# MLA stage: the second retention pair's weights and the first output columns loaded from ScalarE's DMA queue instead of SyncE's

## What is computed

```python
h = _rms_norm(x, attn_norm[layer])
(d_q, d_k, d_v, m_cq, m_ckv, m_krope, r_q, r_k, r_v, r_g) = _split_cols(h @ w_in[layer])
o_diff = _diff_attention(...)      # 4 heads
o_mla = _mla(...)                  # 4 heads: softmax attention over low-rank q, k, v
o_ret = _retention(...)            # 4 heads, in chunks of 128 tokens, with a running state
mixed = jnp.concatenate([o_diff, o_mla, o_ret], axis=-1)
x = x + mixed @ w_out[layer]
h = _rms_norm(x, ffn_norm[layer])
x = x + (jax.nn.silu(h @ w_gate[layer]) * (h @ w_up[layer])) @ w_down[layer]
```

## Time and profile before

| | us |
|---|---|
| median of 3 runs | 2638.94 (2637.67 to 2639.61) |
| the profiled execution: its own time | 2640.68 |
| the profiled execution: span of the profile | 2638.8 |
| PE busy | 2540.5 (96%) |
| DVE, ACT, POOL busy | 1543.5, 1091.1, 1005.8 |

### The profile page before, as it was taken

The page is one execution under the profiler, slowest core; times in us unless marked ns, Lnnn a source line. Parts: engine busy times, 40 slices in busy tenths (PEclk is TensorE's granted clock), DMA queues, the critical chain, the costliest instruction groups (busy, mean ns, idle before and its releaser), DMA issues. The chain is left out here.

```text
span 2638.8 us, 43248 instructions
## 1 busy us (share of the span) xinstructions
PE 2540.5 (96%) x13148; PEld 2179.0 (83%) x13148; DVE 1543.5 (58%) x3050; ACT 1091.1 (41%) x2507; POOL 1005.8 (38%) x1149
## 2 busy tenths in 40 slices
PE   6999989999999999999999999999999999999997
PEld 5999977878788888888889998777887888888886
DVE  4667555472655455577757765555637445445786
ACT  4444544362522222344444545444534332223444
POOL 3455422174254544301044554223823544451011
PEclk9999999999999999999999999999999999999998
DMA  5111011023232333473341101012222233327533
GB/s 182 29 34 36 19 38 39 21 72 144 72 108 94 101 114 109 154 288 96 95 130 32 35 20 41 6 39 91 97 80 89 79 115 107 112 83 269 190 96 120
DMA packets 238682, 242.68 MB, mean 92 GB/s; under 512 B 27936, under 2 KB 171040, under 8 KB 238496
## 3 DMA queue, kind: packets, MB, share of 16 engines
q1 hardware_dynamic: 237968, 238.34, 28.1%
q10 hardware_dynamic: 528, 2.10, 0.2%
HBM read 172.75 MB, written 67.63 MB: 91 GB/s over the span
## 5 line engine op out<-in xcount | busy, mean ns | idle before, releaser
L2533 POOL TENSOR_TENSOR fw_a_lo<-fw_a_raw,fw_a_hi 128x512 fp32r<-128x512 f32 x132 | 178.6, 1354 | 455.1 <-DVE fw_s_raw L2105 455.1
L2533 POOL TENSOR_TENSOR fw_s_lo<-fw_s_raw,fw_s_hi 128x512 fp32r<-128x512 f32 x176 | 232.2, 1332 | 55.2 <-ACT fw_s_hi L1583 55.2
L745 PE MATMUL banks<-ht_hi,da_hi 128*128 128x512 f32 x496 | 192.9, 389 | 0.0
L745 PE MATMUL banks<-ht_lo,da_hi 128*128 128x512 f32 x496 | 192.9, 389 | 0.0
L745 PE MATMUL banks<-ht_hi,da_lo 128*128 128x512 f32 x496 | 192.9, 389 | 0.0
L745 PE MATMUL banks<-w_diff_hi,ht_hi 128*128 128x384 f32 x512 | 179.6, 351 | 2.3 <-DVE dv L1816 2.0
L745 PE MATMUL banks<-w_diff_hi,ht_lo 128*128 128x384 f32 x512 | 171.9, 336 | 0.0
L745 PE MATMUL banks<-w_diff_lo,ht_hi 128*128 128x384 f32 x512 | 171.6, 335 | 0.0
L2361 POOL TENSOR_TENSOR qk_rot<-rope_a,rope_b 128x512 f32<-128x512 f32 x64 | 82.5, 1292 | 195.0 <-DVE rope_b L1802 175.7
L1837 DVE TENSOR_REDUCE stats<-banks 128x1 f32<-128x1024 f32 (+3 forms) x192 | 138.6, 749 | 30.0 <-PE banks L970 24.1
L1657 ACT ACTIVATE u_two<-u_two 128x512 f32<-128x512 f32 x42 | 26.6, 632 | 280.0 <-DVE u_two L2216 280.0
(11 more groups left out here) (364 smaller groups left out, 7481.0 us busy)
## 6 DMA issues: line engine op xcount, KB each, us to landing
da_raw<-act_scratch SPq DMA_DIRECT2D x154, 256.0 KB, 2.6
fw_a_raw<-in_w_gate_dram SPq DMA_DIRECT2D x88, 256.0 KB, 3.1
act_scratch<-act_s SPq DMA_DIRECT2D x66, 256.0 KB, 3.0
w_diff_raw<-in_w_in_dram SPq DMA_DIRECT2D x24, 512.0 KB, 6.4
fw_a<-in_w_up_dram SPq DMA_DIRECT2D x44, 256.0 KB, 3.2
fw_a_raw<-in_w_up_dram SPq DMA_DIRECT2D x44, 256.0 KB, 2.9
act_scratch<-act_zero SPq DMA_DIRECT2D x44, 256.0 KB, 2.4
act_scratch<-act_one SPq DMA_DIRECT2D x44, 256.0 KB, 2.8
```

What stands on the lines that cost most here:

```text
L745: mm = pe.matmul(bank, lhsT, rhs, start=first and i == 0, stop=last and i == len(pairs) - 1, skip_group_check=resumes)
L2533: pool.tensor_tensor(w[1][:], w[2][:], w[0][:].bitcast(F32), ALU.subtract).then_inc(S["f_lo"], 1)
```

## The change

The loads of the second pair's weights and of the first output columns leave SP's stream and stand in ACT's, in `ret_take_z`, between its wait for `z_done` and the copy to `r_z` that used to follow it at once. SP keeps the three small loads, which move from behind the store of unit 25 to behind that of unit 28, and `load_out(1)`, written out.

```diff
-                def load_out(c):
-                    arrives(w_o[c][2][:], w_out[L].rearrange("(k p) n -> p k n", p=P)[:, :, c * 512:(c + 1) * 512],
-                            f"w_in{c}")
...
-                        if h * T + T - 1 - t == 9:
-                            sp.wait_ge(S["z_done"], L * PER["z_done"] + Z_RET + T)
-                            load_ret(1)
-                        if h * T + T - 1 - t == 25:
+                        if h * T + T - 1 - t == 28:
                             sp.wait_ge(S["z_done"], L * PER["z_done"] + Z_UNITS)
-                            load_out(0)
                             arrives(causal[:], causal_dram, "ret_in")
...
                         act.wait_ge(S["z_done"], L * PER["z_done"] + Z_RET + n + 1)
+                        if n == T - 1:
+                            load_second_pair()
+                        if n == RET_UNITS - 1:
+                            load_first_output_columns()
                         act.activation(r_z[n][:], banks[:, Z_BANK, :], ACT.Copy).then_inc(S["z_free"], 1)
+
+                def load_second_pair():
+                    columns = w_in[L].rearrange("(k p) n -> p k n", p=P)
+                    for i in range(4):
+                        begin = COL_RET + i * RET_W + P
+                        act.dma_start(w_ret[2][:, :, i * P:(i + 1) * P], columns[:, :, begin:begin + P]).then_inc(S["w_in0"], 16)
+
+                def load_first_output_columns():
+                    act.dma_start(w_o[0][2][:], w_out[L].rearrange("(k p) n -> p k n", p=P)[:, :, 0:512]).then_inc(S["w_in0"], 16)
```

More of the change, by code:

```diff
@@ L624, in _ @@
                 sp.sem_inc(S["passed"], 1)
-                load_out(1)
+                arrives(w_o[1][2][:], w_out[L].rearrange("(k p) n -> p k n", p=P)[:, :, 512:D], "w_in1")
                 sp.wait_ge(S["x_saved1"], L * PER["x_saved1"] + 16)
```

## The result

| | before | after |
|---|---|---|
| median, same chip, 7 runs each | 2637.97 (2633.37 to 2639.61) | 2657.86 (2642.90 to 2701.24) |
| the profiled execution: its own time, span | 2640.68, 2638.8 | 2645.90, 2644.1 |
| PE, DVE, ACT, POOL busy | 2540.5, 1543.5, 1091.1, 1005.8 | 2541.1, 1542.1, 1091.0, 1004.4 |

The account below looks back on a forecast made before the run. It took a chain through all engines to set the pace where PE waits or is clocked down. +8.1 for the issues less 4.0 for freed stores gave +4.1 on 2638.94: 2643.0 us, range 2636.8 to 2647.0.

Parts of the forecast that it names:

- Part 1: Four DMAs on ACT before unit 7's copy delay the MLA chain in both layers: +8.1 us, bounds 7.0 and 10.3.
- The 0.54 us that the first layer was to get back: First layer's w_ret_hi no longer waits 0.54 us for its DMA, so 3.75 us of delay becomes 3.2.
- Rivals A and C: A: four issues on ACT cost 1.9 us, 2637.8, chance 0.15. C: copy late by 0.48 at most, about 2633.9, chance 0.07.
- Part 2: End of MLA stage: stores no longer wait behind large loads, PE's last turn back comes sooner: -4.8 us, -4.0 net.
- Rival D: Stores share DMA engines with the 2 MB load and land as late as before: +8.1 us, 2647.0, chance 0.08.
- What it gives back: Small loads ahead of the stores of units 29 to 31 may delay reading mixed_rows: 0.4 us per layer set against the gain.
- 1.1 us for one such stretch: Cost of one low-clock stretch, from last turn back to first inner product: 4.58 us in first layer, 3.47 in second.
- The clock behind step 15: PE's added idle time over 3 us likely brings the second layer a low-clock stretch too: 1.1 us.
- rival B: One more low-clock stretch in both layers around step 15 to 17, reading back 0.9 per layer: +7.3, 2646.2, chance 0.18.
- the last clause: Sign that the prediction is wrong: the clock stays down for longer than one stretch.

Follow-up runs that it names:

- e4: Changed kernel with 14 more keep_clock matmuls in step 15, ahead of PE's wait for the copy; 2655.16 us, ratio 1.0092.
- e3: Changed kernel with the second pair's loads back on SP, so only the output columns on ACT, small loads still at unit 28; 2647.13 us, ratio 1.0028.
- e2: Changed kernel with only the second pair's loads on ACT; output columns and small loads back on SP at unit 25; 2648.02 us, ratio 1.0037.
- e9: Changed kernel with gn_w and gn_b loaded behind mixed_rows and causal on its own semaphore; 2643.64 us, ratio 1.002.
- e10: As e9, with the second pair's loads back on SP, so only the output columns on ACT; 2632.79 us, ratio 0.9986.
- e11: As e3, with 9 more keep_clock matmuls ahead of PE's wait for mixed_rows; 2637.17 us, ratio 0.9995.
- e1: The changed kernel run again without any edit; 2671.93 us, ratio 1.0107 against the kernel before.
- e7: Kernel before with only causal, gn_w and gn_b moved from the store of unit 25 to that of unit 28; 2671.79 us, ratio 1.0108.
- e8: Changed kernel with 9 more keep_clock matmuls ahead of PE's wait for mixed_rows; 2646.70 us, ratio 1.0021.
- e5: Changed kernel with gn_w and gn_b loaded behind mixed_rows, causal still sharing their semaphore; 2716.75 us, ratio 1.0301.
- e6: As e5, with the second pair's loads back on SP; 2705.43 us, ratio 1.0272.

## Why the prediction was wrong

**Part 1 (forecast +8.1, bounds 7.0 and 10.3): right.** The four issues took 4.00 us against 3.95 taken. The Trainium skill, "DMA: Bandwidth & Descriptors", § Issuing engines are not separate DMA queues, calls such a time usually small beside the DMA itself; for these loads it is not, on either engine. It builds up from one to the next: on ACT the first of the four took 0.39 us, no more than the one transfer of the output columns (0.38), and the last 1.48; on SP it was 0.39 and 1.46. From the copy of unit 6, which the change does not touch, to the first product with the second pair's weights it was 34.41 us in the first layer before (426.09 to 460.50) and 36.89 after (426.16 to 463.05): +2.5 where 3.2 were forecast. In the second layer 32.73 (1725.32 to 1758.05) became 36.78 (1726.61 to 1763.39): +4.05 where 4.85 were. The delay of the chain can be read without the clock: in e4, whose clock is 1.00 throughout, the same way takes 36.53 and 36.57 us (423.23 to 459.76, 1722.73 to 1759.30), in e3, without the issues, 32.73 and 32.70 (423.35 to 456.08, 1717.53 to 1750.23). That is 3.8 and 3.9 us per layer where 3.75 were forecast. The 0.54 us that the first layer was to get back is not among it; the first layer's smaller shift comes from the kernel before, whose low clock at 447 to 451 had cost it 1.7 us (34.41 against 32.73). So this size came out near 3.2 by luck. By e2's median the whole part costs 9.9 us. The difference between e9 and e10 (+5.4 and -5.4), which differ in this part alone, says 10.8, just over the upper bound. The sum of the two layers' shifts is 6.5 to 7.2 us in the traces (e2: +2.8 and +4.4). Of the 9.3 us by which e2's span is the longer, another 3.4 lie between the layers, where the change touches nothing: from the first product with the output columns in the first layer to the copy of unit 6 in the second it is 1158.71 us (570.53 to 1729.24) against 1155.30 (570.02 to 1725.32), and e2's clock is low there at 1330 to 1338 and 1655 to 1662, that of the kernel before nowhere. Such stretches come and go between traces (e11, without loads of the pair on ACT, has two, e10 one), so one trace of each does not show that the change brings them. Rivals A and C fell with the 4.00 us. (The bound of 10.3 counts one low stretch in each layer beyond the one that the 8.1 have already in the second; one new one in each would make 9.2.)

**Part 2, the stores free of the large loads (-4.8 before what it gives back): right in size, wrong in one premise.** PE's last turn back no longer waits; e10, with nothing given back, measured -5.4 (by its interval -1.3 to -6.1). Rival D fell by its time, but its reason was sound: beside the load of 2 MB from the other queue the stores of units 25 and 26 took 6.0 and 5.6 us to land, not the 1.5 that the forecast took for unit 26 (in the kernel before those of 26 and 27, behind the load, took 8.1 and 6.2). The load now starts 1.4 us before the store of unit 25 and not 0.6 after it, and POOL waits 1.66 and 1.78 us in place of 6.15 once.

**What it gives back: the step that failed.** "I set 0.4 us per layer against this." The chain itself stood in the prediction, in the right order: the small loads ahead of the store of unit 29, that store holding unit 31's tile, this the reading of `mixed_rows`, "no slack". It was sized too small, and was priced as time alone. In the trace PE waits 1.65 and 1.55 us, four times as much. I had the store of unit 28 at about 529, so 531.5 with the shift of 2.5 us; it went as the last of SP's four stores, over at 525.13 + 8.90 = 534.0, because POOL's tile of unit 28 had waited for the store of unit 26, and the three small loads and the store of unit 29 went behind it. This alone would have stayed inside the range: with 1.6 us per layer in place of 0.4 the sum is +8.1 - 4.8 + 3.2 = +6.5, 2645.4. What took the kernel out of it is the second price of the wait, that of the clock: "The price is in rows: ... 1.1 us for one such stretch" came from a place where large products follow at once. In the retention the clock stayed down for 18 to 69 us, in the traces that caught it; at e1's 0.4 us for each that is 7 to 28 us per layer. From the first inner product to the first product with the output columns the first layer takes 30.54 us before, 31.31 in the first trace of the changed kernel and 42.91 in e1 (537.00 to 579.91). With part 1 and part 2 as forecast and this term gone the kernel measures +5.4 (e9; forecast for the whole +4.1); e7, which has this term and neither of the others, measures +32.2. e8, which keeps the late reading but fills the wait, measures +7.1. The rest of the changed kernel's loss is this term.

**The clock behind step 15.** It fell in both layers, for 4 us in each of the first trace (438 to 442, 1739 to 1743), the stretch standing in place of the former one in the first layer (447 to 451). So the sum had it; rival B, one more in each layer, did not come in this trace, though the stretches of e1 and e2 are longer. e4 took it away in both, and nothing of the spread went with it.

The range failed in the same place: its upper end was that of part 1 without part 2, and no case had a stretch of low clock longer than one. Under "what would make the prediction wrong" the last clause named it.

## What to carry to other kernels

When a queue is relieved, follow the last transfer in it to its first reader and compare its landing time with the reader's lead; here 12.1 us of lead against 11.7 of landing meant that 2 us of small loads ahead of it undid a gain of 5. When a load moves to another queue, do not take for the stores beside it the landing time of an idle queue: here 6.0 us and not 1.5. Price a wait of TensorE by the clock behind it too: waits of 1.5 to 1.85 us in the retention cost 7 to 28 us per layer where the clock stayed down, while issues, wait and low clock in the MLA stage cost 6.0 us per layer at most (38.74 less 32.70, e1), and only some executions show it. So run a kernel often enough before believing its profile: one trace of a short execution fitted the forecast, and the loss was in the others.

## What the runs showed of the hardware

- Waits of PE for `mixed_rows` and the clock behind them, by layer: 1.73, 1.85 (e1), 1.80 (e3), 1.64 (e4), 1.53, 1.50 (e7) were followed by 1.2 GHz, at the earliest during the wait (e7, second layer) and at the latest 2 us behind it; 1.65, 1.55 (after), 1.40 (e4) and 0.57 (e3) were not. The same wait does it in one execution and not in another; this is the spread. What decides it stays open. One execution in 73 of the kernel before was long too (2660.60 us at a mean clock of 0.984, beside the runs of e5 to e8); there is no trace of it.
- PE was busy 98 to 100% in the low stretches of e1, e3 and e7, with small products and `keep_clock` matmuls among them, and this did not raise the clock. In e3, e5, e6 and e7 it came back within 2 us of the first 128x512 product with the output columns (598.13 in e5, 1868.28 in e3, the clock at 1.00 from 599 and 1869 on). That is no rule: in e4 it rose nearly 7 us before that product (1866 against 1872.69), in e1 38 and 39 us after it (618 against 579.91, 1949 against 1909.56).
- In the MLA stage PE's idle time of 3.46 us, over twice the wait for `mixed_rows`, was followed by a low clock of 4 us in each layer of the first trace (436 to 444 at a mean of 0.79), of 7 in e2 and of up to 11 in e1 (436 to 447) and e5 (1765 to 1776), and never by one of the length seen in the retention. Scores of up to 128x512 follow there; that the size of the products makes the difference is not shown, since no run changed it.
- Stores of 32 KB landed in 1.5 us at the median of the changed kernel, and in 6.0 and 5.6 us when they were issued 1.4 and 3.9 us behind a load of 2 MB on the other queue (after, first layer; second layer 6.0 and 5.5).
